# A router that turns its blocks of x in another order

## The reference, cut to what matters

```
h2 = _modulate(_rms(x, norm2_g[l]), sh2, sc2)          # h * (1 + scale) + shift
x  = x + g2 * _expert_choice(h2, *moe_w)

_expert_choice(h, w_r, w_g, w_u, w_d):
  # affinities = softmax(h @ w_r) over 16 experts
  # each expert takes the 128 positions with the highest affinity: gate, idx
  # xe = h[idx]; a = xe @ w_g; u = xe @ w_u
  # ye = (silu(a) * u) @ w_d * gate
  # the ye are added up at their positions
```

## Time and profile before

| | us |
|---|---|
| median of three runs | 2206.61 (2205.09 to 2208.05) |
| profiled execution, its own time | 2207.18 |
| its span, first to last instruction | 2205.1 |
| PE busy | 2135.7 (97%) |
| DVE busy | 1634.9 (74%) |
| ACT busy | 1124.4 (51%) |
| POOL busy | 188.8 (9%) |
| mean granted TensorE clock | 0.988 of full |

### The profile page before, as it was taken

How to read it: one execution, slowest core, us unless ns; L and a number is a source line. 1 busy time by engine, 2 the same in 40 slices (tenths; PEclk the granted TensorE clock), 3 DMA queues, 4 the chain that set the end, 5 groups by cost and what they waited for, 6 DMA issues and landing times.

```text
span 2205.1 us, 28128 instructions
## 1 busy us (share of the span) xinstructions
PE 2135.7 (97%) x10948; PEld 1783.4 (81%) x10948; DVE 1634.9 (74%) x2537; ACT 1124.4 (51%) x1725; POOL 188.8 (9%) x270
## 2 busy tenths in 40 slices
PE   7999899999999999989999999899999999899997
PEld 6888787888888888868888888788888885688885
DVE  7777558999887987986344263688887746699996
ACT  6777435444443434444322242577776212588884
POOL 0001100000001000000110032000000000111111
PEclk9999999999999999999999999999999999899998
DMA  4122713555469998652343112000002603999996
GB/s 152 49 68 75 269 67 123 202 181 180 173 240 405 380 340 280 214 128 76 124 143 100 39 48 83 11 1 1 1 20 73 247 29 153 359 392 380 381 385 209
DMA packets 114548, 373.99 MB, mean 170 GB/s; under 512 B 13376, under 2 KB 13664, under 8 KB 112752
## 3 DMA queue, kind: packets, MB, share of 16 engines
q1 hardware_dynamic: 86544, 273.00, 33.7%
q0 software_dynamic: 26720, 95.01, 13.1%
q10 hardware_dynamic: 1152, 4.19, 0.5%
HBM read 302.94 MB, written 69.21 MB: 169 GB/s over the span
## 4 chain that ended last, share of the span: by engine, by line
PE 83%; DVE 10%; ACT 4%; issue 1%; DMA 1%; POOLq 0%; SPq 0%; ACTq 0%; DVEq 0%
PE psum L99 24%; PE psum L100 24%; PE psum L101 24%; PE psum L3046 3%; PE psum L3057 2%; DVE w_lo L281 1%; PE psum L1017 1%; ACT MP_hi L3147 1%; DVE small L3193 1%; DVE MP_lo L3240 1%; ACT PB L3113 1%; PE psum L990 1%; PE psum L3886 1%; PE psum L3613 1%; DVE idx L3586 1%
## 5 line engine op out<-in xcount | busy, mean ns | idle before, releaser
L272 ACT ACTIVATE w_hi<-rawe 128x1024 fp32r<-128x1024 f32 x211 | 217.8, 1056 | 151.4 <-PE psum L101 73.6
L99 PE MATMUL psum<-U_hi,w_hi 128*128 128x512 f32 x688 | 271.0, 394 | 13.4 <-DVE w_lo L281 10.7
L281 DVE TENSOR_TENSOR w_lo<-rawe,w_hi 128x1024 fp32r<-128x1024 f32 x211 | 249.7, 1220 | 37.6 <-ACT w_hi L272 36.9
L100 PE MATMUL psum<-U_lo,w_hi 128*128 128x512 f32 x688 | 269.0, 391 | 0.0
L101 PE MATMUL psum<-U_hi,w_lo 128*128 128x512 f32 x688 | 268.7, 391 | 0.0
L281 DVE TENSOR_TENSOR w_lo<-raw,w_hi 128x1024 fp32r<-128x1024 f32 (+2 forms) x175 | 194.7, 1122 | 88.4 <-ACT w_hi L272 88.1
L272 ACT ACTIVATE w_hi<-raw 128x1024 fp32r<-128x1024 f32 (+2 forms) x176 | 169.0, 967 | 93.1 <-PE psum L101 48.5
L99 PE MATMUL psum<-B_hi,w_hi 128*128 128x512 f32 x448 | 175.3, 391 | 2.6 <-DVE w_lo L281 2.6
L101 PE MATMUL psum<-B_hi,w_lo 128*128 128x512 f32 x448 | 174.3, 389 | 0.0
L100 PE MATMUL psum<-B_lo,w_hi 128*128 128x512 f32 x448 | 174.3, 389 | 0.0
L99 PE MATMUL psum<-w_hi 128*128 128x512 f32 x448 | 174.3, 389 | 0.0
(11 more groups left out here) (490 smaller groups left out, 5088.5 us busy)
## 6 DMA issues: line engine op xcount, KB each, us to landing
rawe<-in_w_e SPq DMA_DIRECT2D x112, 512.0 KB, 17.2
rawe<-in_w_dn SPq DMA_DIRECT2D x70, 512.0 KB, 6.5
rawx<-in_w_e SPq DMA_DIRECT2D x56, 512.0 KB, 17.5
rawe<-ta SPq DMA_DIRECT2D x43, 512.0 KB, 7.2
ta<-cbuf SPq DMA_DIRECT2D x64, 256.0 KB, 2.4
raw<-in_w_dn SPq DMA_DIRECT2D x26, 512.0 KB, 6.8
ta<-rg SPq DMA_DIRECT2D x48, 256.0 KB, 2.0
raw<-in_w_e SPq DMA_DIRECT2D x24, 512.0 KB, 17.2
```

The costliest lines, as they stand in the source:

```text
L99: e.matmul(o, l[0], r[0], start=first, stop=False, skip_group_check=skip)
L100: e.matmul(o, l[0], r[1], start=False, stop=False, skip_group_check=skip)
L272: act.e.activation(hi, src, ACT.Copy).then_inc(w_hi, 1)
L281: dve.e.tensor_tensor(lo, src, f(hi), ALU.subtract).then_inc(w_lo, 1)
```

## The change

The order of the sixteen rows becomes 8 to 15, then 0 to 7 (`ROWS`), on PE, ACT and POOL. The buffer of a row goes by its place in this order. Row 8 moves ahead of the turn of the logits on PE, and ahead of Exp on ACT; row 9 moves ahead of the turn of the affinities on PE, and behind the copy of bB on ACT. `dg2` is made ahead of the softmax on DVE; PE's "g2" follows the turn of the affinities and comes before the other fourteen rows, ACT's copy to g2b behind row 9. The Silu that brings in the table follows it. The rawx slots now wait for row 7, PE's last. The gather waits until the writes of all sixteen rows have landed, row 7's the last of them, instead of those of the first eight. What is computed does not change.

```diff
@@ -3490,54 +3490,64 @@
-    lt_b, bB_b, af_b = next_banks(), next_banks(2), next_banks()
-    rt.pe.plan(("bw",), ("logits", 0), ("logits", 1), ("turn",), ("bB",), ("aff",))
-    rt.dve.plan(*[(x,) for x in ("bw", "dgB", "dgA", "r", "dgS", "cb", "lgT", "byr", "plus", "max", "sub", "sum", "inv",
-                                 "aff", "cur")])
-    rt.act.plan(("lgT",), ("exp",), ("bB",))
-    row_b = []
-    for r in range(16):
-        row_b.append(next_banks(2))
+    ROWS = [*range(8, 16), *range(8)]
+    rt.pe.plan(("bw",), ("logits", 0), ("logits", 1))
+    rt.dve.plan(*[(x,) for x in ("bw", "dgB", "dgA", "r", "dgS", "dg2", "cb", "lgT", "byr", "plus", "max", "sub", "sum",
+                                 "inv", "aff", "cur")])
+    rt.act.plan(("lgT",), ("row", 8), ("exp",), ("bB",))
+    row_b = {8: next_banks(2)}
+    lt_b, bB_b = next_banks(), next_banks(2)
+    row_b[9] = next_banks(2)
+    af_b, g2_b = next_banks(), next_banks(2)
+    rt.pe.plan(("row", 8), ("turn",), ("bB",), ("row", 9), ("aff",), ("g2",))
+    rt.act.plan(("row", 9), ("g2",))
+    for r in ROWS[2:]:
+        row_b[r] = next_banks(2)
         rt.pe.plan(("row", r))
         rt.act.plan(("row", r))
...
-    top_b, g2_b = next_banks(), next_banks(2)
-    rt.pe.plan(("top",), ("g2",))
+    top_b = next_banks()
+    rt.pe.plan(("top",))
     rt.dve.plan(("vrev",), ("idxf",), ("irev",), ("tops",), ("gcol",), ("pick",), ("step",), ("picked",), ("icf",),
-                ("icol",), ("dg2",))
-    rt.act.plan(("g2",))
+                ("icol",))
     sm8, su8 = small[:, 0:8], small[:, 8:16]
...
     def router_pool(pool):
-        for r in range(16):
+        for i, r in enumerate(ROWS):
             pool.wait_ge(*rt.act("row", r))
             dst = A["h2s"] if r < 8 else out
             n = r % 8
-            pool.e.dma_start(dst[n * P:n * P + P, :], row[r % 5][:]).then_inc(row_out[r % 5].sem, 16)
+            pool.e.dma_start(dst[n * P:n * P + P, :], row[i % 5][:]).then_inc(row_out[i % 5].sem, 16)
+
+    def row_act(act, i):
+        r = ROWS[i]
+        act.wait_ge(*rt.pe("row", r))
+        if i > 4:
+            act.wait_ge(*row_out[i % 5].at(i // 5))
+        scale = r4[:, r:r + 1] if r < 8 else 1.0
+        act.e.activation(row[i % 5][:], two(row_b[r]), ACT.Copy, scale=scale).then_inc(*rt.act.one("row", r))
 
     def router_act(act):
         act.wait_ge(*rt.pe("logits", 0))
         act.e.activation(lgT[0:16, half(0)], bank(lg_b)[0:16, :], ACT.Copy).then_inc(*rt.act.one("lgT"))
+        row_act(act, 0)
         act.wait_ge(*rt.dve("sub"))
         act.e.activation(aff[:], aff[:], ACT.Exp).then_inc(*rt.act.one("exp"))
         act.wait_ge(*rt.pe("bB"))
         act.e.activation(bB[:], two(bB_b), ACT.Copy).then_inc(*rt.act.one("bB"))
-        act.e.activation(vec[:, 127:128], EPSV, ACT.Silu)
-        for r in range(16):
-            act.wait_ge(*rt.pe("row", r))
-            if r > 4:
-                act.wait_ge(*row_out[r % 5].at(r // 5))
-            scale = r4[:, r:r + 1] if r < 8 else 1.0
-            act.e.activation(row[r % 5][:], two(row_b[r]), ACT.Copy, scale=scale).then_inc(*rt.act.one("row", r))
-        make_hi(act, T_E0 + 3)
+        row_act(act, 1)
         act.wait_ge(*rt.pe("g2"))
         act.e.activation(g2b[:], two(g2_b), ACT.Copy).then_inc(*rt.act.one("g2"))
+        act.e.activation(vec[:, 127:128], EPSV, ACT.Silu)
+        for i in range(2, 16):
+            row_act(act, i)
+        make_hi(act, T_E0 + 3)
 
...
         e.tensor_tensor(dgS[:], ident_rows(8), by_block(sd4, 8), ALU.mult).then_inc(*rt.dve.one("dgS"))
+        e.tensor_tensor(dg2[:], ident_rows(8), by_block(GT2, 8), ALU.mult).then_inc(*rt.dve.one("dg2"))
...
         e.tensor_copy(icol[:], icf[:]).then_inc(*rt.dve.one("icol"))
         make_lo(dve, T_E0 + 3)
-        e.tensor_tensor(dg2[:], ident_rows(8), by_block(GT2, 8), ALU.mult).then_inc(*rt.dve.one("dg2"))
+
+    def row_pe(pe, r):
+        n = r % 8
+        claim(pe, row_b[r], 2)
+        if r == 0:
+            pe.wait_ge(*rt.dve("dgS"))
...
+        for k in range(8):
+            o, x = two(row_b[r])[:, k * P:k * P + P], X[:, k, n * P:n * P + P]
+            if r < 8:
+                if k % 4 == 0:
+                    pe.e.matmul(bank(row_b[r] + k // 4), dgS[:, n, :], bB[:, half(k // 4)], start=True, stop=False,
+                                skip_group_check=True)
+                m = pe.e.matmul(o, x, dgA[:, k, :], start=False, stop=k % 4 == 3, skip_group_check=True)
+            else:
+                m = pe.e.transpose(o, x, ident[:])
...
@@ -3631,6 +3659,7 @@
             logits(k)
         hand_over(lg_b, 1, rt.act("lgT"))
         hand_over(lg_b + 1, 1, rt.dve("lgT"))
+        row_pe(pe, 8)
         claim(pe, lt_b)
         pe.wait_ge(*rt.act("lgT"))
         pe.wait_ge(*rt.dve("lgT"))
...
         hand_over(bB_b, 2, rt.act("bB"))
+        row_pe(pe, 9)
         claim(pe, af_b)
         pe.wait_ge(*rt.dve("aff"))
         for n in range(4):
@@ -3653,29 +3683,6 @@
                                ident[:])
         m.then_inc(*rt.pe.one("aff"))
         hand_over(af_b, 1, rt.dve("cur"))
...
-        claim(pe, top_b)
-        pe.wait_ge(*rt.dve("irev"))
-        for i, x in enumerate((vals, idxf, vrev, irev)):
-            m = pe.e.transpose(psum[:, top_b, 32 * i:32 * i + 32], x[0:32, :], ident[0:32, 0:32])
-        m.then_inc(*rt.pe.one("top"))
-        hand_over(top_b, 1, rt.dve("tops"))
         claim(pe, g2_b, 2)
         pe.wait_ge(*rt.dve("dg2"))
         for i in range(2):
@@ -3683,6 +3690,14 @@
                             start=True, stop=True)
         m.then_inc(*rt.pe.one("g2"))
         hand_over(g2_b, 2, rt.act("g2"))
+        for r in ROWS[2:]:
+            row_pe(pe, r)
+        claim(pe, top_b)
+        pe.wait_ge(*rt.dve("irev"))
+        for i, x in enumerate((vals, idxf, vrev, irev)):
+            m = pe.e.transpose(psum[:, top_b, 32 * i:32 * i + 32], x[0:32, :], ident[0:32, 0:32])
+        m.then_inc(*rt.pe.one("top"))
+        hand_over(top_b, 1, rt.dve("tops"))
 
...
     for i in range(8):
-        slot_freed[N_RAW + 15 + i] = [rt.pe("row", 15)]
+        slot_freed[N_RAW + 15 + i] = [rt.pe("row", 7)]
...
@@ -3762,7 +3777,7 @@
         else:
             pool.wait_ge(*rt.pe("row", 7))
             for k in range(5):
-                pool.wait_ge(*row_out[k].at(2 if k < 3 else 1))
+                pool.wait_ge(*row_out[k].at(4 if k == 0 else 3))
         pool.wait_ge(*rt.dve("icol"))
```

More of the change, by code:

```diff
@@ L3606, in router_dve @@
         make_lo(dve, T_E0 + 3)
-        e.tensor_tensor(dg2[:], ident_rows(8), by_block(GT2, 8), ALU.mult).then_inc(*rt.dve.one("dg2"))
+    def row_pe(pe, r):
[3 more added lines that the diff above has]
+            pe.wait_ge(*rt.dve("dgS"))
+            pe.wait_ge(*rt.act("bB"))
+        for k in range(8):
[7 more added lines that the diff above has]
+                m = pe.e.transpose(o, x, ident[:])
+        m.then_inc(*rt.pe.one("row", r))
+        hand_over(row_b[r], 2, rt.act("row", r))
     def router_pe(pe):
```

## The result

The changed kernel takes 2211.61 us (median of 22 runs, 2207.10 to 2213.51), the kernel before in the same series 2207.28 (22 runs, 2204.52 to 2211.98): a ratio of 1.0017, 95% interval 1.0011 to 1.0023. That is 3.75 us slower, between 2.4 and 5.1. The profiled execution took 2210.01 us for a span of 2208.1. The busy shares are as before (PE 97%, DVE 74%, ACT 51%, POOL 9%).

The account below looks back on a forecast made before the run. PE bounds the kernel behind its first transposes, so time follows the landing of expert 0's gathered rows. Wait for row 7 +1.4, gather length 0, clock 0, all else 0, on 2206.61, gives 2208.0 us; range 2204.5 to 2211.5.

Parts of the forecast that it names:

- no measurable change: Whole kernel: a difference within 0.2%, or 4.4 us, of the kernel before; chance 0.87.
- near side of the forecast: Whole kernel: with the forecast itself, a time +0 to +3 us against the kernel before; chance 0.58.
- rival 2: Expert 0's gather: weight loads get in front, it takes 9.8 us, lands +4.2; 2212.5 us with the clock; chance 0.10.
- three signs of being wrong: Profile: table load still at 1844.3, gather starting before 1889.6, or gather landing in under 5.5 us or over 9.
- The softmax: ACT, ahead of Exp: the table load stands behind row 8's copy, so Exp comes 0.55 us later.
- it swallows Exp's 0.55: Sum of terms: the gather's +1.4 us wait for row 7, in place of icol, absorbs Exp's 0.55 us delay.
- The rows: PE and ACT beside the search: row 0 starts at 1857.2, ACT copies row 7 at 1885.5, "top" not held up.
- The gather's new wait: POOL: expert 0's gather waits for row 7's write, not icol, and starts at 1890.4, 1.4 us later.
- The gather's length: Expert 0's gather: 7.0 us as before, difference 0 (-3.7 to +2.8), between bounds of 3.3 and 9.8.
- rival 1: Expert 0's gather: little traffic, takes 3.3 us, lands 2.3 us earlier than before; 2204.3 us; chance 0.17.
- g2 off the tail gives nothing: Tail on PE and DVE: removing g2 and dg2 gains 0, since the gather hid them.
- The clock: PE behind its first transposes of gathered rows: half clock as before, difference 0, within 1.7 us either way.

Follow-up runs that it names:

- e1: The changed kernel with ACT's copy of row 8 moved behind Exp; 2210.51 us, 1.0012 of the kernel before.
- e3: The changed kernel with the Silu, and so its table load, behind ACT's copy of row 7; 2211.59 us, 1.0014 of the kernel before.
- e2: The changed kernel with rows in the order 8, 9, 0 to 7, 10 to 15, the gather waiting for the normed rows alone; 2209.04 us, ratio 1.0010.
- e4: The changed kernel with SP's loads from the eleventh rawe tile on held until expert 0's gathered rows have landed; 2207.30 us, 0.9996 of the kernel before.
- e9: The kernel before with the gate row g2 alone moved ahead of the rows; 2210.44 us, 1.0012 of the kernel before.
- e0_after: The changed kernel run again unaltered, as reference on the chip of three other kernels; 2211.88 us, 1.0019 of the kernel before.
- e5_three: The changed kernel with the edits of e1, e3 and e4 together; 2207.04 us, 0.9997 of the kernel before.
- e13_before_fill: The kernel before with useless matmuls on PE around g2, 14 ahead and 10 behind; 2206.37 us, 0.9991 of the kernel before.
- e10: e5_three plus 26 useless matmuls in PE's wait for the gathered rows; 2207.01 us, 0.9989 of the kernel before.
- e6: e5_three plus 60 useless matmuls in PE's wait for the gathered rows; 2211.11 us, 1.0012 of the kernel before.
- e11: The changed kernel plus 40 useless matmuls between the turn of the search's results and the gathered rows; 2213.05 us, 1.0021 of the kernel before.

## Why the prediction came out as it did

The forecast was 2208.0 us, +1.4, no measurable change, in a range of 2204.5 to 2211.5. The direction and the place are right and the size is too small; "no measurable change" holds only by the prediction's own measure of 0.2%: +3.75 us by the ratio, which from the median that the forecast went by (2206.61) is 2210.4, inside the range and above the forecast. In the longer series both medians are higher, and the changed kernel's own, 2211.61, lies 0.1 above the range. The loss also lies above the near side of the forecast (up to +3, 0.58) and below rival 2's full price of +4.2; none of the three signs of being wrong came.

- **The softmax: right.** Exp +0.55 was forecast, +0.56 measured; the load is behind the copy, at 1847.44, and Exp follows its end within 0.02 us. So the drain of some 1380 ns that the Trainium skill adds (ScalarE: Activation LUTs, What ACT_TABLE_LOAD costs) is not there; the load's 1283 ns agree with the 1.28 measured. What was wrong is "it swallows Exp's 0.55": e1 shows that Exp's delay runs through to row 7. The working had it in (it began g2 from the delayed affinities), the sentence on the sum denied it.
- **The rows: right.** First matmul of row 0 forecast 12.65 behind the logits (1857.2), measured 12.37; row 7's copy 40.95 against 40.68. That ACT's chain with the Silu holds the rows up is true for 0.4 us only (e3).
- **The gather's new wait: right.** Start +1.4 forecast, +1.35 measured. POOL took 0.79 from row 7's landing, not 0.6. The prediction put this time down to the waits that stand in the text behind that landing. But in the kernel before the chain has the same 0.79 behind icol, the last wait in the text, and in e2 it has 0.80: the waits are not what it is made of.
- **The gather's length: the term that was mis-sized.** I put 7.0 and a difference of 0; it is 8.4 and 8.1, so +1.1 to +1.4. This is rival 2's mechanism: the loads released by the same landing go ahead. e4 prices it at 4.0 us of the gather and 4.6 us of time. The bounds, 3.3 and 9.8, held both values; the row to take was the third gather, 8.5, with the loads running ahead of it, and the prediction had its price, +2.9. The lower bound of 3.3 was 1 us too low: even with the queues free the gather takes 4.3 to 4.4, so rival 1 could never have won its 2.3 us whole. The 3.2 us that rival 1 takes, as an estimate, from the Trainium skill (DMA: Bandwidth & Descriptors, Anatomy of one DMA) fit the write of row 7 (2.9) better than this gather, of whose 4.4 us 1.02 are POOL's issue.
- **g2 off the tail gives nothing: right**, and e9 shows that alone it costs.
- **The clock: right in the profile.** 0 was put, within 1.7. From PE's start on the gathered rows the changed kernel has

```profile
1899.63:1906.30 6.67, 6.07 (x18) 4.83 (x19) 1.42 (x3) 2.25 (x3) 0.94 (x1) 0.51 1.02 413
```

so some 6.5 us at half, where it was 6.1 before: 0.2 us lost.

- **What the trace leaves over.** Start and length make PE begin 2.4 to 2.7 us later, and from there to the end of the span it takes 0 to 0.5 us less; the ratio says 3.75 (2.4 to 5.1). In the 22 runs the time goes with the mean granted clock: 2207.1 at 0.989, 2209.2 and 2209.6 at 0.987, 2210.0 to 2211.8 at 0.986 (the profiled one among them, 2210.0), 2212.4 to 2213.5 in the nine at 0.985. That doesn't settle it: the kernel before spreads as widely (0.984 to 0.989 in the 35 runs beside e0_after), and I have no profile of a run at 0.985. (Later rises do occur: e9's profile has 7.7 us at half from PE's start on the rows.) But the gap is not peculiar to the new order. Add up, for each row of the table, what PE's start and the rest of the span differ from the kernel before's, and put the ratio beside it: e2_h2_first -0.4 and +2.2, e5_three -1.7 and -0.7, e9_gate_only +0.2 and +2.7, e13_before_fill -3.4 and -2.0. The last two keep the old order. In twelve of the thirteen profiles the ratio says more than the moments do, by 0.1 to 2.6 us. The one profile of the kernel before also reaches the end of the logits earliest of all fourteen, and its run took 2207.18 us; the medians of that kernel are 2207.28 in the first series and 2208.3 to 2208.9 in the later ones. So a likely reason is that this one profile shows a good run of the kernel before. With a single profile of it that is not shown, and this part, 1 to 1.5 us, stays open.

## What to carry to other kernels

When a step is moved off a busy tail, look at what its completion releases: here one landing let go both the transfer on the critical path and a stream of loads that had no hurry, and the loads got ahead. Hold the loads that can wait behind the transfer that can't; that was worth more (4.6 us) than any of the moves. A wait of the bounding engine costs its own length and the slow clock behind it, so filling it can pay (2 to 2.4 us in e13 and e10), as long as the filling is no longer than the wait (e6), reaches up to its end (e11), and is priced from a row of the same instruction.

## What the runs showed of the hardware

An indirect gather of 128 rows of 4 KB lands 4.3 to 4.4 us after its issue with the queues free, 6.0 to 7.3 behind writes of its own queue, 8.1 to 8.7 with the loads of another queue released just ahead of it. This is nearly a factor of two, and it has two parts: the first packets move 4.7 us after the issue in place of 1.6, and then the gather has half of the transfers. The Trainium skill (DMA: Bandwidth & Descriptors, Queues, rings and completion order) says that each DMA engine goes round between the queues that have work. The even shares, 0.73 MB of one queue and 0.70 of the other in 3.5 us of the changed kernel, agree with that; the late first packets are not explained by it or by a run here. A table load on ACT stood behind whatever copies were ahead of its function, took 1.28 us, and the function followed it within 0.02 us. A matmul of 128 columns in f32 was issued as two instructions and took 0.22 us at the full clock, where a transpose of the same shape took 0.11. The low stretch of the clock from PE's first transposes of the gathered rows on (6.1 to 7.7 us at half) was gone when useless matmuls filled PE's wait up to its end, and with it 2.1 us of the span in e10 against e5 and 3.0 in e13 against the kernel before.
